# Expert groups ranked by token count, with the two smallest in one window of 128 slots

## What is computed

```python
p_grp = softmax(t @ w_rg + b_rg); g_val, g_idx = top_k(p_grp, 1)      # each token picks one group of four
le_sel = take_along_axis(le.reshape(n, 4, 4), g_idx[:, :, None], 1)   # the logits of its group's 4 experts
e_val, e_idx = top_k(softmax(le_sel), 2)                              # and two experts in it
e_val = e_val / sum(e_val)
gate = sum(one_hot(g_idx * 4 + e_idx, 16) * (g_val * e_val)[..., None], axis=1)
act = silu(einsum('nd,edf->nef', t, w_e_gate)) * einsum('nd,edf->nef', t, w_e_up)   # f = 256
out = einsum('nef,efd->nd', act * gate[:, :, None], w_e_down)
```

## Time and profile before

| | |
|---|---|
| median of 3 executions | 977.29 us (977.1 to 977.81) |
| profiled execution, its own time | 977.7 us |
| its span | 975.9 us |
| PE busy | 961.4 us, 99% |
| DVE busy | 761.5 us, 78% |
| ACT busy | 528.7 us, 54% |
| POOL busy | 42.1 us, 4% |
| TensorE clock granted | 0.996 of 2.4 GHz |
| DMA | 178.41 MB, 183 GB/s on average |
| chain that ended last | PE 88%, DVE 9%, DMA 1%, ACT 1% |

### The profile page before, as it was taken

The page is one execution under the profiler, slowest core; times in us unless marked ns, Lnnn a source line. Parts: engine busy times, 40 slices in busy tenths (PEclk is TensorE's granted clock), DMA queues, the critical chain, the costliest instruction groups (busy, mean ns, idle before and its releaser), DMA issues.

```text
span 975.9 us, 16871 instructions
## 1 busy us (share of the span) xinstructions
PE 961.4 (99%) x6638; PEld 884.7 (91%) x6638; DVE 761.5 (78%) x1148; ACT 528.7 (54%) x764; POOL 42.1 (4%) x42
## 2 busy tenths in 40 slices
PE   9999999999999999999999999999999999999997
PEld 7999999999999888888889999887999898999996
DVE  5699998899757887788868777976385389787876
ACT  4545545734444666677754635563555476555544
POOL 0002002001102000000001000000100120000000
PEclk9999999999999999999999999999999999999999
DMA  8955646265530777877964434122453256555541
GB/s 302 339 165 179 207 163 205 102 233 194 171 108 1 274 261 265 320 277 283 325 238 130 174 100 160 65 72 85 169 184 120 87 194 211 178 192 193 179 167 43
DMA packets 49602, 178.41 MB, mean 183 GB/s; under 512 B 5632, under 2 KB 5888, under 8 KB 49280
## 3 DMA queue, kind: packets, MB, share of 16 engines
q1 hardware_dynamic: 47952, 172.51, 51.5%
q10 hardware_dynamic: 1584, 4.99, 1.4%
HBM read 176.43 MB, written 1.05 MB: 182 GB/s over the span
## 4 chain that ended last, share of the span: by engine, by line
PE 88%; DVE 9%; DMA 1%; ACT 1%; issue 1%; SPq 0%; DVEq 0%; ACTq 0%
PE psum L723 86%; DVE wl L2189 3%; DVE work L2189 1%; DMA raw<-stream_in 1%; DVE xl L2227 1%; DVE memn L2189 1%; PE psum L965 1%; ACT wh L1687 1%; PE psum L1272 0%; DVE work L3026 0%; DVE xh L2222 0%; DVE rstd L2217 0%; DVE xT L2189 0%; DVE ypair L2311 0%; DVE ypair L2189 0%
## 5 line engine op out<-in xcount | busy, mean ns | idle before, releaser
L1687 ACT CAST wh<-raw 128x1024 fp32r<-128x1024 f32 x302 | 313.7, 1051 | 285.8 <-PE psum L723 267.9
L2189 DVE TENSOR_TENSOR wl<-raw,wh 128x1024 fp32r<-128x1024 f32 x302 | 362.4, 1234 | 66.2 <-ACT wh L1687 63.2
L723 PE MATMUL psum<-xh,wh 128*128 128x256 f32 x1024 | 290.4, 284 | 2.9 <-DVE wl L2189 2.6
L723 PE MATMUL psum<-xl,wh 128*128 128x256 f32 x1024 | 287.0, 280 | 0.0
L723 PE MATMUL psum<-xh,wl 128*128 128x256 f32 x1024 | 286.7, 280 | 0.0
L723 PEld LDWEIGHTS psum<-xh,wh 128*128 128x128 f32 x1024 | 193.6, 189 | 6.3 <-issue 2.7
L723 PEld LDWEIGHTS psum<-xl,wh 128*128 128x128 f32 x1024 | 193.7, 189 | 0.6
L723 PEld LDWEIGHTS psum<-xh,wl 128*128 128x128 f32 x1024 | 193.6, 189 | 0.0
L723 PE MATMUL psum<-wh,slots 128*128 128x512 f32 x320 | 101.7, 391 | 0.0
L723 PE MATMUL psum<-yh,wh 128*128 128x256 f32 x256 | 72.1, 282 | 0.5 <-DVE wl L2189 0.5
L723 PE MATMUL psum<-yl,wh 128*128 128x256 f32 x256 | 71.5, 279 | 0.0
(11 more groups left out here) (285 smaller groups left out, 1522.2 us busy)
## 6 DMA issues: line engine op xcount, KB each, us to landing
raw<-stream_in SPq DMA_DIRECT2D x325, 512.0 KB, 4.5
memn<-mem_t_in ACTq DMA_DIRECT2D x2, 1024.0 KB, 9.5
out_rows<-work SPq DMA_DIRECT2D x4, 256.0 KB, 2.2
const<-const_in ACTq DMA_DIRECT2D x1, 581.0 KB, 4.9
xT<-x_t_in SPq DMA_DIRECT2D x2, 256.0 KB, 4.8
xT<-x_t_in ACTq DMA_DIRECT2D x2, 256.0 KB, 5.6
raw<-stream_in SPq DMA_DIRECT2D x2, 256.0 KB, 5.7
mask<-mask_in ACTq DMA_DIRECT2D x1, 512.0 KB, 14.0
```

What stands on the lines that cost most here:

```text
L723: return nc.tensor.matmul(out, w, x, start=start, stop=stop, **kw)
L1687: nc.scalar.copy(wh[:, SLOT[c], :], raw[:, c % RAW, :]).then_inc(hi_ready, 1)
L2189: return v.tensor_tensor(out, a, b, op)
```

## The change

All four groups are now ranked by their number of tokens (ties by number). The two smallest, places 0 and 1, share window 0: the smallest takes the first slots and the second follows it. Together they never have more than 128 of 256 tokens. Place 2 has window 1, place 3 windows 2 and 3, and `slots`, `slot_of`, `back` and the gathers shrink to four windows. The gates of window 0 are kept twice, masked: once for the slots below the smallest group's count, once for those from it on. So an expert of place 0 gives zero in the slots of place 1, and the eight experts of both places add up in the same two banks with no split between them. The number of passes stays at 20.

```diff
-SLOTS = 5 * P
+SLOTS = 4 * P
 def windows(p):
-    return (p,) if p < 3 else (3, 4)
+    return (max(p - 1, 0),) if p < 3 else (2, 3)
...
-        back = at("back", X_AT, [P, 5, T], F32R)
+        back = at("back", X_AT, [P, 4, T], F32R)
...
-            return slots[:, j % 2, j // 2, P:SLOTS], psum[:, j % 4, :]
+            return slots[:, j % 2, j // 2, P:SLOTS], psum[:, j % 4, 0:SLOTS - P]
...
                 for t in range(TT):
-                    last = matmul(psum[:, j % 4, :], x[:, t, k * P:(k + 1) * P], slot_of[:, t, P:SLOTS],
+                    last = matmul(psum[:, j % 4, 0:SLOTS - P], x[:, t, k * P:(k + 1) * P], slot_of[:, t, P:SLOTS],
                                   t == 0, t == TT - 1)
...
                 pe.wait_ge(gates_ready, 1)
-                for w in range(5):
+                for w in range(4):
...
-                    if w == 4:
+                    if w == 3:
                         last.then_inc(gates_summed, 1)
                     if w:
                         gather_other(w + 3)
+                gather_other(7)
...
-                elif p and p < 3 and j == 0:
-                    pe.wait_ge(y_split, p)
+                elif p == 2 and j == 0:
+                    pe.wait_ge(y_split, 1)
...
-                                         j == 0 and f == 0, j == 3 and f == 1)
+                                         j == 0 and f == 0 and p != 1, j == 3 and f == 1 and p != 0)
...
-                pe.wait_ge(y_split, max(w + 1, 3))
+                pe.wait_ge(y_split, max(w + 1, 2))
...
-            for w in range(5):
+            for w in range(4):
                 scatter(w)
...
-                if n and EXPERT_ORDER[n - 1][1] == 3:
+                if n and EXPERT_ORDER[n - 1] in ((1, 3), (2, 3)):
                     sum_high(EXPERT_ORDER[n - 1][0], n - 1)
...
-            link(v.tensor_reduce(cmax, count, AX_X, ALU.max))
-            link(tt(big, count, cmax.to_broadcast([P, 4]), ALU.is_equal))
-            link(tt(big, big, prio[:, 0, :], ALU.mult))
-            link(v.tensor_reduce(big_at, big, AX_X, ALU.max))
-            link(tt(big, big, big_at.to_broadcast([P, 4]), ALU.is_equal))
-            link(tt(big2, big, mc("group", 4), ALU.mult))
-            link(v.tensor_reduce(big_at, big2, AX_X, ALU.add))
-            link(v.tensor_scalar(order, mc("group", 4), big_at, None, ALU.is_ge))
-            link(tt(order, order, mc("group", 4), ALU.add))
-            link(v.tensor_copy(order[:, 3:4], big_at))
+            link(v.scalar_tensor_tensor(size, count, 4.0, mc("tie", 4), ALU.mult, ALU.add))
+            link(tt(larger[:], size.unsqueeze(2).to_broadcast([P, 4, 4]), size.unsqueeze(1).to_broadcast([P, 4, 4]),
+                    ALU.is_gt))
+            link(v.tensor_reduce(rank, larger[:], AX_X, ALU.add))
+            link(tt(larger[:], mc("group", 4).unsqueeze(2).to_broadcast([P, 4, 4]),
+                    rank.unsqueeze(1).to_broadcast([P, 4, 4]), ALU.is_equal))
+            link(tt(larger[:], larger[:], mc("group", 4).unsqueeze(1).to_broadcast([P, 4, 4]), ALU.mult))
+            link(v.tensor_reduce(order, larger[:], AX_X, ALU.add))
             v.tensor_copy(order_i[:], order).then_inc(order_ready, 1)
-            tt(big2, big, mc("to_last", 4), ALU.mult)
-            link(v.tensor_scalar(past, mc("group", 4), big_at, None, ALU.is_gt))
-            link(v.scalar_tensor_tensor(start, past, -float(P), mc("base", 4), ALU.mult, ALU.add))
-            link(tt(start, start, big2, ALU.add))
+            v.tensor_reduce(least, count, AX_X, ALU.min)
+            link(v.tensor_scalar(start, rank, -1.0, 0.0, ALU.add, ALU.max))
+            link(v.tensor_scalar(second, rank, 1.0, least, ALU.is_equal, ALU.mult))
+            v.tensor_scalar(shared[:, 0:1], mc("row", 1), least, None, ALU.is_lt)
+            v.tensor_scalar(shared[:, 1:2], mc("row", 1), least, None, ALU.is_ge)
+            link(v.scalar_tensor_tensor(start, start, float(P), second, ALU.mult, ALU.add))
...
-                    link(v.tensor_copy(gslot[:], psum[:, 4, T:T + 20].rearrange("p (w e) -> p w e", w=5)))
-                for q, w in enumerate(windows(p), q0):
+                    slot_gates = psum[:, 4, T:T + 16].rearrange("p (w e) -> p w e", w=4)
+                    for i in range(2):
+                        v.tensor_scalar(gslot[:, i, :], slot_gates[:, 0, :], shared[:, i:i + 1], None, ALU.mult)
+                    link(v.tensor_copy(gslot[:, 2:5, :], slot_gates[:, 1:4, :]))
+                for q, w in enumerate((p,) if p < 3 else (3, 4), q0):
...
-                    for w in range(5):
+                    for w in range(4):
                         last = v.tensor_scalar(back[:, w, :], psum[:, 4, 0:T], mc("row", 1, w), None, ALU.is_equal)
```

More of the change, by code:

```diff
@@ L199 @@
 _at = 0
-for _name, _n in (("slot", SLOTS), ("earlier", P), ("bias", 20), ("group", 4), ("base", 4), ("to_last", 4), ("row", 5)):
+for _name, _n in (("slot", SLOTS), ("earlier", P), ("bias", 20), ("group", 4), ("tie", 4), ("row", 4)):
     MOE[_name] = _at
@@ L376, in build @@
         g4b = r(TT, 4)
-        cmax = r(1)
-        big = r(4)
-        big2 = r(4)
-        big_at = r(1)
-        past = r(4)
+        least = r(1)
+        size = r(4)
+        larger = r(4, 4)
+        rank = r(4)
+        second = r(4)
         start = r(4)
+        shared = r(2)
         order = r(4)
@@ L1257, in up_and_gate @@
                             pe.wait_ge(hid_split, q - 1)
-                        if h == 3 and p == 3 and w == 4:
+                        if h == 3 and p == 3 and w == 3:
                             last.then_inc(first_done, 1)
@@ L1301, in scatter @@
                         last = matmul(out, slots[:, h, o, w * P:(w + 1) * P], back[:, w, :],
-                                      w == 0 and o % 2 == 0 and h == 0, w == 4 and h == 1, skip_group_check=True)
-                    if w == 4 and o % 2:
+                                      w == 0 and o % 2 == 0 and h == 0, w == 3 and h == 1, skip_group_check=True)
+                    if w == 3 and o % 2:
                         last.then_inc(sum_done, 1)
@@ L3226, in _moe_constants @@
     put("group", np.broadcast_to(g, (P, 4)))
-    put("base", np.broadcast_to(P * g, (P, 4)))
-    put("to_last", np.broadcast_to(P * (3 - g), (P, 4)))
-    put("row", p + P * np.arange(5)[None, :])
+    put("tie", np.broadcast_to(3 - g, (P, 4)))
+    put("row", p + P * np.arange(4)[None, :])
     return c
```

## The result

The changed kernel took **972.07 us** (median of 6 runs, 971.38 to 973.6). The kernel before, in 6 runs beside it, took 977.37 us (977.1 to 978.24). The profiled execution took 971.38 us with a span of 969.5 us.

What follows compares the result with a forecast made beforehand. PE was taken as the bound, so removed matmul time shortens the run: 1.2 us up to the transposes, 0.93 for gathers behind them and 1.87 for the scatter make 4.0, from 977.29 to 973.3 us; range 972.3 to 975.1.

Steps and rivals of the forecast that it cites:

- Gathers: 32 gather matmuls go from 512 to 384 columns, 232.5 to 174.6 ns each, saving 1.85 us.
- Rival B: A gather's pace is not set by its width, so 384 columns step like 512: 975.0 us; chance 0.07.
- the price by the Trainium skill: A line through the skill's figures: gathers save only 0.53 us, a scatter matmul costs 98 ns; whole change near 2.5 us.
- Scatter: 80 scatter matmuls become 64 at 116.8 ns each, saving 1.87 us, with no wait for results.
- D: The gain is absorbed behind the scatter, where weights or normalisation set the time: 977.3 us; chance 0.03.
- First turned tile: Where hidden tiles are first turned, transposes start 1.2 us sooner; PE saves 1.38 us and 0.2 is given back.
- Rival A: Front bound by ACT and weights: group order no sooner, less gain before the transposes; 973.7 to 974.5 us; chance 0.10.
- At nothing: Parts priced at zero: slot comparison, fewer DVE and ACT operations, the wait for group 0's sum, smaller constants' DMA.
- C: The gathered tile's rows of 512 columns slow weight loads; at 256 ns a load 12.5 us more, 985.8 us; chance 0.03.
- The sum: 1.2 us up to the transposes, 0.93 for 16 gathers behind them, 1.87 for the scatter: 4.0 us.
- the base: The time of the kernel before from which the saving was subtracted: median 977.29 us; its profiled execution took 977.7 us.
- 0.3 for the spread of the runs: Allowance for run variation in the range's lower end, 972.3 us.

Runs made afterwards that it cites:

- 512-column edit: The changed kernel with its 32 gather matmuls 512 columns wide again, the first 128 columns unused: 973.88 us.
- five-window edit: The changed kernel with window 0 scattered twice, so 80 scatter matmuls as before the change: 974.77 us.
- slow-rank edit: The changed kernel with four more linked DVE copies in the chain that ranks the groups: 973.32 us.
- doubled rows: The changed kernel with each of the second layer's 20 ten-row head-row matmuls issued twice: 976.84 us.
- full height: Head-row matmuls over 128 partitions, zeros below the heads: kernel before 975.54 us, changed kernel 971.26 us, changed kernel also with gates one DVE weight step earlier 971.07 us.
- early gates: The changed kernel with the first expert's gates taken by DVE ahead of its third weight subtraction, not behind it: 972.95 us.
- fifth round: The changed kernel with a fifth round of gate sums and the old order of the last gathers: 973.3 us.

## Why the prediction was wrong, step by step

- **Gathers.** Forecast 174.6 ns each, measured 174. Right. Rival B and the price by the Trainium skill, "TensorE: Matmul & The Clock Gate", section "Back-to-back issue gap" (about 81 ns at 128 columns, 131 at 512 in a sustained stream), are both refuted here by the eight gathers and by the 512-column edit; the trace has 112 and 232.5 ns at these widths.
- **Scatter.** 1.87 us forecast; 9.34 - 7.47 = 1.87 measured, and again in the five-window edit. Nothing was absorbed behind it (D), since 4.85 us at its end are still 4.85 us at 537.48.
- **First turned tile.** Transposes 1.2 us sooner, forecast; 1.10 measured, with PE standing 0.71 us by the profile (forecast 0.5 to 0.8). The forecast counted its 0.47 us of standing before from the step of the last gathers; the profile has 0.22 there. By the forecast's count PE now stands 0.88 us (338.13 - 336.90 less two gathers), so that PE saved 1.5 us and gave 0.4 back, where 1.38 and 0.2 were forecast. The steps behind it held: order chain 0.78 us shorter (forecast 0.8), first transfer 0.78 us sooner behind the anchor, four 384-column copies of ACT at 491 ns (forecast 483), subtraction as the last thing ahead of the gates. The queue's move was forecast at nearly 0.8 us, and the subtraction starts 0.74 us sooner. But it does not all come from the order: by the slow-rank edit only half of the order's time reaches this point. The four shorter copies (0.42 us) can be the rest; no experiment takes them apart. DVE's small operations take 337.59 - 337.13 = 0.46 us to the multiplication, where one copy took 0.21: 0.25 us more and not 0.1. The point came out 0.1 us off in sum. Rival A needed dearer steps on 16 elements: they cost 0.20 to 0.21 us like the others.
- **At nothing.** The wait for group 0's sum was priced at nothing; beyond the 1.10 us at the turn and the 0.93 of the gathers the trace is 0.11 us ahead when the last hidden tiles are turned (501.55 - 498.57 less 0.84 is 2.14). That is within what traces of one kernel differ by (0.14 us in the change's five, 0.29 in the three of before), so that it makes good what the turn lacked is chance as far as is known. Expert matmuls kept their pace (639 in the 141 us of the long stretch, 638 before), which refutes C.
- **The sum.** 4.0 us forecast; 4.01 us in the trace between anchor and scatter, 3.97 between the means of eight traces, 3.9 between medians at like clock over 79 runs, 4.1 and 4.3 in two batches. The sum was right.
- **What failed** is the last sentence of the first part, "nothing in the change lets PE rest longer, so the clock gives and takes nothing", together with the base and the "0.3 for the spread of the runs". The change does indeed not let PE rest longer, but the base carried a cost of the clock that other executions do not have. I looked at the clock in the two stretches of the earlier trace rows alone. The profiled execution's clock of 0.996 was in the table, and part of its cause, 3.4 us at 1.2 GHz at 565 us, was in the trace, in a layer that the change does not touch. A clock of 0.997 or less comes in about half of the executions of before (31 of 68) and is worth 1.6 us. The three runs of before lay at 977.1 to 977.8, where the 37 runs of the high clocks have their median at 975.94 and their highest at 977.56; their own clocks are not on record but for the profiled one, so I infer them from the times. The six runs of the change have the low clock in two cases only (0.997, 973.6 us). 977.37 - 972.07 = 5.3 is thus 3.9 to 4.1 for the change, and 1.2 to 1.4 for the mix of executions. A range that reached down to 977.29 - 4.0 - 1.6 = 971.7 us would have held the result. Why all six runs of before had it stays open: at 31 of 68 that is a chance of about one in a hundred. The share differs between batches (6 of 19, 7 of 20, 18 of 29), and even at 18 of 29 it is one in seventeen.
- The doubled rows show what brings the stretch in this place, and at full height it is in none of the three kernels' traces. That every fall of the clock is gone with it is not shown, as 5 of the 22 runs at full height have 0.997. Nor did the change itself make the stretch rarer: counting the change and its five edits that leave the 20 matmuls as they are (gathers, scatter, early gates, slow rank, fifth round), 24 of 50 runs have 0.997 or less, the same share as 31 of 68.

**What stays open.** At like clock the full-height kernels lie 0.9 us below theirs as well (975.26 against 976.19 in the same batch, 971.14 against 972.06), and I have no row for it; the kernel before itself moved from 976.19 to 975.51 at like clock between two batches, which ran on different chips, so it may be the runs' own. The fifth-round edit had, in its profile, the lower clock in another place, behind 0.55 and 0.76 us of PE standing near 771 to 773 us; I did not follow it. What makes 5 of the 22 runs at full height read 0.997 has no trace. The 0.84 us between the two traces ahead of the anchor were not traced further either, but they need no cause in the change: the anchors of the twelve executions of the experiments lie between 301.92 and 303.07.

## What to carry to other kernels

Before summing a change of a few microseconds, read the granted clock over the whole span, not only where the edit is: in this kernel a mean below that of other runs was a stretch at half clock somewhere in all six such traces, and it came and went between executions. Price it, ask in how many of the runs shown it may be, and let the range hold both answers. And measure a change behind an anchor in the trace that it cannot touch, in more than one trace: pairs gave 3.79 to 4.22 us there, while two pairs of medians gave 5.3 and 4.1.

Matmuls with a few rows that broadcast a small table are worth trying at full height with zeros, since here it cost no time on PE (2.38 us for 20 against 2.37). Where PE waits on a chain through several engines' queues, part of each saving is given back: 0.84 us of delay in DVE's chain moved PE by 0.40, and 0.79 us of delay in PE's own gate sums by 0.30.

## What the runs showed of the hardware that I had not expected

- TensorE's clock fell to the 1.2 GHz level without a rest of PE: what stood ahead was 2.3 us of matmuls with 10 rows on both operands, PE being 5.00 of 5.00 us busy in both windows. Behind 20 of them it fell in some executions, for 3.4 us in each of the four traces that show it; with 40 the mean clock was low in all twelve, and the one trace has it low for some 6.8 us. I had watched only for idle PE. The Trainium skill, "TensorE: Matmul & The Clock Gate", Part 1, says that the chip gates this clock by how busy PE has been, and that one kernel can differ from run to run in how long it stays low at its start. No trace here has a low clock at the start (1.00 in the first 10 us of before), but the mean of one and the same kernel differs from run to run (0.994 to 0.999 in 68 runs of before). As to the first, the profile's busy time does not tell the two cases apart: PE is busy alike with operands of 10 rows and of 128.
- The same matmuls at 128 rows take the same time (2.38 us for 20, 2.37 with 10 rows), and no run with them had a clock under 0.997 (22 runs of three kernels, five of them at 0.997), where 22 of the 68 runs of before had.
- At 512 columns the pace of load and matmul is 232.5 ns, at 384 it is 174, at 256 it is 117 and at 128 it is still 112: proportional to the width from 256 up, and hardly less below.
